# The second norm's modulation and the first two weight units of the MLP in halves of 256 tokens

## The reference, cut to what matters

```python
h = _modulate(_rms_norm(x, norm2_g), shift2, scale2)   # rms over 2048 features, times norm2_g, * (1 + scale2) + shift2
y = jnp.square(jax.nn.relu(h @ w_mlp1)) @ w_mlp2       # 2048 -> 8192 -> 2048
return x + gate2[:, None, :] * y
```

## Time and profile before

| | us |
|---|---|
| three runs: lowest, median, highest | 2652.95, 2655.0, 2656.99 |
| the profiled execution: span of its trace | 2652.9 |
| PE, matmuls in flight (share of the span) | 2431.0 (92%) |
| POOL | 1180.6 (45%) |
| DVE | 1017.4 (38%) |
| ACT | 722.7 (27%) |
| chain that ended last, share of PE | 74% |

### The profile page before, as it was taken

How to read it: one execution, slowest core, us unless ns; L and a number is a source line. 1 busy time by engine, 2 the same in 40 slices (tenths; PEclk the granted TensorE clock), 3 DMA queues, 4 the chain that set the end, 5 groups by cost and what they waited for, 6 DMA issues and landing times.

```text
span 2652.9 us, 27413 instructions
## 1 busy us (share of the span) xinstructions
PE 2431.0 (92%) x10822; PEld 1999.2 (75%) x10822; DVE 1017.4 (38%) x1397; ACT 722.7 (27%) x974; POOL 1180.6 (45%) x570
## 2 busy tenths in 40 slices
PE   3759887899788989998999999999999999999999
PEld 2558666777676778876888888888888888888887
DVE  4973469754244536767311211203122112131221
ACT  4222242333332332213222212213122122131222
POOL 2534346545665543343444444444444444444442
PEclk6868798899988999998999999999999999999999
DMA  8673345544555455221222222222232332322321
GB/s 318 218 275 116 123 139 166 177 162 167 194 164 170 159 171 189 97 95 64 95 95 95 95 95 95 95 95 96 95 97 95 102 101 92 99 105 92 102 103 57
DMA packets 184671, 342.08 MB, mean 129 GB/s; under 512 B 5361, under 2 KB 32148, under 8 KB 183828
## 3 DMA queue, kind: packets, MB, share of 16 engines
q1 hardware_dynamic: 175968, 336.78, 37.7%
q10 hardware_dynamic: 8628, 4.28, 0.6%
HBM read 324.26 MB, written 16.78 MB: 129 GB/s over the span
## 4 chain that ended last, share of the span: by engine, by line
PE 74%; DVE 10%; DMA 6%; issue 5%; POOL 4%; ACT 2%; SPq 0%; ACTq 0%; DVEq 0%; POOLq 0%
PE pj L1222 41%; PE pa L1222 27%; DMA ada<-w_ada_in 4%; DVE acc L802 2%; POOL acc L701 2%; POOL w_lo L680 2%; PE pa L1226 1%; PE pa L1279 1%; DVE sq L1198 1%; PE pa L1292 1%; DVE acc L1034 1%; PE pa L1411 1%; DVE score L942 1%; DMA resid<-xT_dram 1%; PE pa L1433 1%
## 5 line engine op out<-in xcount | busy, mean ns | idle before, releaser
L680 POOL TENSOR_TENSOR w_lo<-raw,w_hi 128x1024 fp32r<-128x1024 f32 (+1 forms) x396 | 952.6, 2406 | 1251.6 <-ACT w_hi L462 1251.6
L462 ACT ACTIVATE w_hi<-raw 128x1024 fp32r<-128x1024 f32 (+1 forms) x396 | 416.7, 1053 | 1517.5 <-PE pj L1222 971.4
L1222 PE MATMUL pj<-h,w_hi 128*128 128x512 f32 x1664 | 526.4, 398 | 9.5 <-DVE h L1096 4.7
L1222 PE MATMUL pj<-w_hi,h 128*128 128x512 f32 (+1 forms) x1536 | 500.8, 404 | 28.0 <-DVE rot L993 10.1
L1222 PEld LDWEIGHTS pj<-h,w_hi 128*128 128x128 f32 x1664 | 316.9, 192 | 80.3 <-issue 9.6
L1222 PEld LDWEIGHTS pj<-w_hi,h 128*128 128x128 f32 x1536 | 302.6, 200 | 98.5 <-issue 19.2
L1198 DVE TENSOR_TENSOR sq<-relu 128x512 f32<-128x512 f32 x64 | 160.5, 2508 | 518.9 <-ACT relu L636 518.9
L1222 PE MATMUL pa<-h,w_hi 128*128 128x512 f32 x1152 | 357.6, 392 | 0.0
L1222 PE MATMUL pj<-h,w_lo 128*128 128x512 f32 x832 | 328.9, 395 | 0.0
L1222 PE MATMUL pj<-mid,w_hi 128*128 128x512 f32 x1024 | 317.8, 391 | 5.6 <-DVE mid L1202 5.6
L1222 PE MATMUL pa<-mid,w_hi 128*128 128x512 f32 x1024 | 316.1, 390 | 0.0
(11 more groups left out here) (163 smaller groups left out, 1900.1 us busy)
## 6 DMA issues: line engine op xcount, KB each, us to landing
raw<-w_mlp_in SPq DMA_DIRECT2D x64, 2048.0 KB, 8.2
ada<-w_ada_in SPq DMA_DIRECT2D x128, 512.0 KB, 4.5
raw<-w_in_in SPq DMA_DIRECT2D x22, 2048.0 KB, 10.1
ada_first<-w_ada_in SPq DMA_DIRECT2D x32, 1024.0 KB, 6.1
raw<-w_out_in SPq DMA_DIRECT2D x8, 2048.0 KB, 8.1
ret<-ret_dram SPq DMA_DIRECT2D x32, 256.0 KB, 4.0
raw<-w_in_in SPq DMA_DIRECT2D x4, 1792.0 KB, 12.3
x_nat<-x_in SPq DMA_DIRECT2D x4, 1024.0 KB, 7.5
```

The lines of the kernel that those rows point to most:

```text
L462: act.activation(split_chunk(w_hi, u, j), raw_chunk(u, j), ACT.Copy).then_inc(hi_done, 1)
L680: pool.tensor_tensor(split_chunk(w_lo, u, j), raw_chunk(u, j), split_chunk(w_hi, u, j).bitcast(F32), ALU.subtract).then_inc(lo_done, 1)
L1222: last = pe.matmul(dst, lhs[a], rhs[b], start=start and n == 0, stop=stop and n == 2)
```

## The change

The modulation goes by half tiles of 256 tokens, 32 steps in this order: first half of h tiles 0 to 7, second half of tiles 0 to 7, first half of tiles 8 to 15, second half of tiles 8 to 15 (`half_of`). PE's units 0 and 1 of step 0 go by halves too: first all four chunks of the unit with the first 256 tokens, then all four with the others; a chunk is released (`chunk_used`) after its second half. Step 0 is written out for this, and PE's loop runs steps 1 to 6. In ACT's program the loop over h tiles becomes one over half tiles, at the same place.

```diff
+    def half_of(n):
+
+        kt = 8 * (n // 16) + n % 8
+        return kt, slice(256 * (n // 8 % 2), 256 * (n // 8 % 2) + 256)
...
             for j in range(4):
                 split_hi(U_MLP, j)
-            for kt in range(KT):
-                act.wait_ge(t2_ready, kt + 1)
-                act.activation(h[:, kt, HI, :], relu[:, kt % 2, :], ACT.Identity,
+            for n in range(2 * KT):
+                kt, half_ = half_of(n)
+                act.wait_ge(t2_ready, n + 1)
+                act.activation(h[:, kt, HI, half_], relu[:, n % 2, half_], ACT.Identity,
                                bias=mod[:, 48 + kt:49 + kt]).then_inc(h2_hi, 1)
...
                 if isinstance(c, int) and c == 0 and n < 2:
-                    act.wait_ge(h2_ready, KT)
+                    act.wait_ge(h2_ready, 2 * KT)
...
-            for kt in range(KT + 1):
-                if kt < KT:
-                    modulate(kt, 1, resid, pa[:, 2, :], relu, 3 * KT, t2_ready, h2_hi, h2_ready, 0)
-                if kt > 0:
-                    modulate(kt - 1, 1, resid, pa[:, 2, :], relu, 3 * KT, t2_ready, h2_hi, h2_ready, 1)
+            for n in range(2 * KT + 1):
+                if n < 2 * KT:
+                    kt, half_ = half_of(n)
+                    need(dve, h2_ready, n - 1)
+                    dve.scalar_tensor_tensor(relu[:, n % 2, half_], resid[:, kt, half_], gain[:, 1, kt:kt + 1],
+                                             pa[:, 2, half_], ALU.mult, ALU.mult).then_inc(t2_ready, 1)
+                if n > 0:
+                    kt, half_ = half_of(n - 1)
+                    dve.wait_ge(h2_hi, n)
+                    dve.scalar_tensor_tensor(h[:, kt, LO, half_], relu[:, (n - 1) % 2, half_],
+                                             mod[:, 3 * KT + kt:3 * KT + kt + 1], h[:, kt, HI, half_].bitcast(F32),
+                                             ALU.add, ALU.subtract).then_inc(h2_ready, 1)
...
+            def half_chunk(q, k0, bank, e, start, stop, count):
+
+                j, cols = q % 4, slice(256 * e, 256 * e + 256)
+                pe.wait_ge(lo_done, q + 1)
+                for kk in range(8):
+                    if j == 0:
+                        pe.wait_ge(h2_ready, count + kk + 1)
+                    last = product(bank[:, cols], [w[:, j, P * kk:P * kk + P] for w in (w_hi, w_lo)],
+                                   [h[:, k0 + kk, s, cols] for s in (HI, LO)], start and kk == 0, stop and kk == 7)
+                if e == 1:
+                    last.then_inc(chunk_used, 1)
+
             def mlp_step(c, final=False):
                 for m in range(4):
                     a, hf = divmod(m, 2)
                     banks = pa if a else pj
+                    if isinstance(c, int) and c == 0 and a == 0:
+                        for e in range(2):
+                            for j in range(4):
+                                if hf == 0 and e == 0:
+                                    pe.wait_ge(added, 24 + j + 1)
+                                half_chunk(4 * (U_MLP + m) + j, 8 * hf, banks[:, j, :], e, hf == 0 and e == 0,
+                                           hf == 1 and e == 1, 16 * hf + 8 * e)
+                        continue
                     for j in range(4):
...
                         features_chunk(4 * (U_MLP + m) + j, h, 8 * hf, banks[:, j, :], hf == 0, hf == 1,
-                                       h2_ready if a == 0 and j == 0 else None, 8 * hf, c)
+                                       None, 0, c)
...
-            with pe.Fori(0, STEPS - 1) as c:
+            mlp_step(0)
+            with pe.Fori(1, STEPS - 1) as c:
                 mlp_step(c)
             mlp_step(STEPS - 1, final=True)
```

## The result

The changed kernel takes 2665.8 us (median of 5 runs, 2660.6 to 2670.9), the kernel before 2653.4 in the same comparison (5 runs, 2652.1 to 2657.0): ratio 1.0048, 95% interval 1.0032 to 1.0065. It is **slower by about 12 us**; 2659.6 and "within 0.2%" were forecast, and the range ended at 2663.5. The profiled execution took 2660.55 us at a span of 2658.8; it is the fastest of the five.

What follows compares the result with a forecast made beforehand. PE, busy 92% of the span, was taken as the bound, with 5.3 us to gain in unit 0's first chunk. Late split +2.3, matmuls +0.3 and clock +2.0 made +4.6 on 2655.0: 2659.6 us, range 2655.5 to 2663.5.

Steps and rivals of the forecast that it cites:

- What costs nothing: PE's loop turns and later units' splits: no added wait; a gap at the added loop entry at most some tenths of a us.
- The last rival: Halves come, but a cover against waits fails or PE's loop entry costs more than tenths: +6 to +8 us; chance 3%.
- Cadence: Modulation on DVE: a half step every 0.90 us, against 1.45 us per whole tile; range 0.88 to 0.92.
- the PSUM row: Profile row for DVE operations also reading PSUM: 692 ns for 512 columns, 420 for 256, so 0.27 us saved per operation.
- The estimate of 0.72 us a half step: Modulation on DVE: pace from the skill's table, used by the rival that operations halve in full, 2651.9 us; chance 5%.
- Late split: ACT's split of unit 1 follows the longer modulation: PE idles 4.4 us and unit 1 starts 2.3 us later.
- Matmuls: Unit 1 on PE: 256-column matmuls at 115 ns each, 22.1 us against 21.76, +0.3 us (0 to +1.2).
- Clock: PE's 4.4 us pause before unit 1 drops its clock to the lower level: +2.0 us, between 1.9 and 3.2.
- Sum at unit 1's end: Late split, matmuls and clock together: +4.6 us at unit 1's end and so at the kernel's end.
- Range: Whole kernel: 2655.5 to 2663.5 us, covering the forecast and the rival in which the clock holds, ends cut a little.
- the clock's rival: PE pauses too shortly before unit 1 to lose its clock: only +2.6 us, 2657.6 us; chance 22%.

Runs made afterwards that it cites:

- e2: Changed kernel plus 204 already-met waits at PE's start, moving its loop by 102 instructions to where it lay before; 2661.5 us, ratio 1.0018.
- e11: Changed kernel measured once more, nothing else altered; 2667.1 us, ratio 1.0056 against the kernel before.
- e6: e2's kernel with unit 1 in whole 512-column matmuls and the loop ending at 0.62 of a packet; one execution, 2659.4 us.
- e10: e7's kernel measured once more, nothing else altered; 2654.5 us, ratio 1.0006 against the kernel before.
- e7: Kernel before with step 0 written out, PE taking unit 0's first six h tiles one by one into all four banks; 2649.5 us, ratio 0.9988.
- e1: Kernel before plus 310 already-met waits at PE's start, moving its loop by 155 instructions; 2668.8 us, ratio 1.0046.
- e8: Kernel before plus 230 already-met waits at PE's start, moving its loop by 115 instructions; one execution, 2654.7 us.

## Why the prediction was wrong

**The step that failed** is in "What costs nothing": both turns of the loop in the trace of before were free, so the turns of the moved loop were put at nothing, and only an added entry was given tenths of a us. The rows are right, and they were read as a property of loops. They were one of a loop at one place. Writing out step 0 and doubling the matmuls of two units moved the loop by 1947 instructions, to a place at which each jump back fetches code again and PE then stands still. The cost was looked for at the entry, once; it came at five jumps back, 1.0 us each in the profile (E - M of 1374.6 against e2's 1369.5) and 1.3 in e11. The last rival ("some cover above fails, or PE's entry costs more than tenths", +6 to +8, 3%) allowed for something unnamed and for too little of it; the mechanism was in no rival. Without the turns' price the change is e2: 5.5 us between the medians and 5.2 by E, where +4.6 was forecast, and 2655.0 x 1.0018 = 2659.8.

Step by step, from the modulation's first operation:

- **Cadence:** 0.90 forecast, 0.91 measured (2 x 0.27 us saved of 1.45, by the PSUM row). Right. The Trainium skill's rule against small tiles (VectorE: DVE Perf Modes, "The TRN2 errata — SBUF-src ops pay a fixed extra latency per instruction") holds here: 0.48 us for 256 columns against 0.75 for 512. The estimate of 0.72 us a half step from its table doesn't.
- **Late split:** unit 1 starts at 1259.37 - 1226.88 = 32.49; forecast 1263.1 - 1231.21 = 31.9. Right in kind, 0.6 short, most of it 31 x 0.013 of cadence. PE's pause was 3.2 us, not 4.4, since unit 0 ended later, at 29.3 and not 27.5: the clock came up 7 to 8 us after PE's start and the matmuls were dearer.
- **Matmuls:** 120 ns, the upper end of the term's range, for the 115 taken. Unit 1 lost 1.3 us by it (23.04 against 21.76), forecast 0.3. e6 shows 1.1. The Trainium skill's 262 cycles (TensorE: Matmul & The Clock Gate, "Back-to-back issue gap"), which it gives for a matmul's isolated gap, are by estimate 109 ns at 2.4 GHz and further off.
- **Clock:** 24.78 - 23.04 = 1.7 us, forecast 2.0. Right in size, but by some luck: the pause was 3.2 us and not the 4.4 from which the fall was argued, and that the fall can come after the pause was not foreseen.
- **Sum at unit 1's end:** +5.8, forecast +4.6. Terms: 2.9 for the start (32.49 against 1260.8 - 1231.21 = 29.6), 1.3 matmuls, 1.7 clock; the three make 5.9. Against the forecast the start and the matmuls came 0.6 and 1.0 us dearer, the clock 0.3 cheaper.
- **What does cost nothing:** units 2 and 3 wait for no split, as said; E without the turns' price is +5.2 (e2), 0.6 less than +5.8, but E - M of the kernels without a gap (before, e2 to e10) lies between 1369.5 and 1370.3 anyway, so the 0.6 is within that scatter.
- **Range:** it is said to have the terms' ends cut a little. By the prediction's own terms they are 2656.7 (the clock's rival with a cadence of 0.88) and 2662.3 (+7.3), so 2655.5 to 2663.5 is wider on both sides, and was missed all the same.

With the turns' 5 to 6 us, 10.2 to 11.4 us by E stand against 12.4 between the medians; the interval of the ratio, 8 to 17 us, holds it.

The change's idea was sound as far as "three matmuls a tile don't fill PE" goes: unit 0 did end earlier, at 29.3 against 29.6. But it gained 0.3 us there, paid 5.8 for it by the split that waits behind a longer modulation and by two units of dearer matmuls, and e7 shows that the stall could be filled without touching the modulation.

## What to carry to other kernels

Where a loop's code moves, look at the instruction queue's packets first: more packets than the code has means that jumps back fetch again, and a stretch of "issue" a few matmuls behind a jump shows whether that costs time. A few waits that are already met, put where the engine idles, can move the loop back. An engine that is late because its operands come slowly is better given other work on the operands it has (more output banks per tile) than smaller pieces. And when an engine's pieces are halved, ask what stands behind them in the program of each engine that handles them.

## What was unexpected of the hardware

- PE's loop of 1596 instructions (6.2 packets of 16.4 KB) is fetched once for all its six or seven turns when it ends at 0.37 to 0.68 of a packet, and in each turn anew (about 9 packets) when it ends at 0.97 or 0.98. The gap comes seven or eight matmuls into the new turn and is 0.4 to 1.2 us long, different each time (changed, e1, e11). In e8, at 0.82, the one refetching left no gap. A shift of 155 instructions alone made the kernel before 0.46% slower.
- The clock fell 0.6 us after the end of a 3.2 us pause, in the stage 1260 to 1263 (granted clock 0.50), and not in the pause, whose last stage has 1.00.
- A matmul of 256 columns with its own load takes 120 ns at full clock, though half of the 512-column one is 113 and one of 80 columns takes 112. That load and columns hide each other less where they are about equally long would fit this; it isn't shown.
